# Transposing attention output and x1 by DMA instead of on TensorE, with the output projection moved ahead among the gates

## The reference, cut to what matters

```
h = x @ W_in + b_in                 # q | k | v | z | gate_attn | gate_gmlp
y_a = SWA_GQA(q, k, v, sinks) @ W_branch_attn
y_b = SGU(gelu(z)) @ W_branch_gmlp
mix = sigmoid(gate_attn) * y_a + sigmoid(gate_gmlp) * y_b
x1  = LayerNorm(alpha * x + mix @ W_out)
y   = LayerNorm(alpha * x1 + relu(x1 @ W_up)^2 @ W_down)
```

## Time and profile before

| | us |
|---|---|
| median of 3 runs | 1052.94 (1052.09 to 1054.36) |
| the profiled execution, slowest core's span | 1045.3 |
| the profiled execution, its own time | 1046.84 |
| spans of the 8 cores | 1043.9 to 1045.3 |
| mean granted TensorE clock of the cores | 0.994 to 0.996 |

### The profile page before, as it was taken

The page is one execution under the profiler, slowest core; times in us unless marked ns, Lnnn a source line. Parts: engine busy times, 40 slices in busy tenths (PEclk is TensorE's granted clock), DMA queues, the critical chain, the costliest instruction groups (busy, mean ns, idle before and its releaser), DMA issues.

```text
span 1045.3 us, 16998 instructions; the slowest of 8 cores (1043.9 to 1045.3 us)
## 1 busy us (share of the span) xinstructions
PE 1023.3 (98%) x6054; PEld 498.9 (48%) x6054; DVE 611.5 (59%) x1087; ACT 360.4 (34%) x484; POOL 89.1 (9%) x152
## 2 busy tenths in 40 slices
PE   8999999999999999999999999999999999999994
PEld 3446455554444444444444645555444444444442
DVE  2866477765876312336787827777486832133476
ACT  0454666651425200330024646666123430023100
POOL 4210000000111000000012000000010100010000
PEclk9999999999999999999999999999999999999998
DMA  9995234241797812953198222542156464086011
GB/s 160 188 174 95 41 53 98 54 102 33 150 162 150 142 20 35 166 82 82 61 185 149 50 41 44 91 102 51 61 124 138 75 129 80 1 134 108 21 61 80
DMA packets 20484, 98.65 MB, mean 94 GB/s; under 512 B 2353, under 2 KB 2993, under 8 KB 11954
## 3 DMA queue, kind: packets, MB, share of 16 engines
q0 software_dynamic: 13344, 73.41, 42.1%
q1 hardware_dynamic: 7058, 24.16, 6.8%
HBM read 162.57 MB, written 8.39 MB: 164 GB/s over the span
## 4 chain that ended last, share of the span: by engine, by line
PE 93%; DVE 3%; DMA 1%; issue 1%; ACT 1%; POOL 0%; DVEq 0%; POOLq 0%; ACTq 0%
PE ps L431 61%; PE ps L1147 20%; PE ps L924 3%; PE ps L674 2%; PE ps L942 2%; PE ps L889 2%; DMA ring<-wz 1%; PE ps L795 1%; DVE scr L392 1%; PE ps L972 1%; PE ps L1063 1%; PE ps L742 1%; DVE scr L897 0%; ACT scr L409 0%; DVE Cg L392 0%
## 5 line engine op out<-in xcount | busy, mean ns | idle before, releaser
L431 PE MATMUL ps<-reg,ring 128*128 128x512 bf16 x1536 | 344.7, 379 | 0.0
L431 PE MATMUL ps<-xT_s,ring 128*128 128x512 bf16 x1120 | 252.2, 375 | 0.2 <-DVE reg L392 0.2
L431 PEld LDWEIGHTS ps<-reg,ring 128*128 128x128 bf16 x1536 | 147.6, 98 | 172.7 <-issue 2.1
L1147 PE MATMUL ps<-ring,reg 128*128 128x512 bf16 x992 | 214.8, 379 | 0.0
L403 ACT ACTIVATE scr<-ps 128x512 f32<-128x512 f32 x128 | 76.4, 597 | 263.4 <-PE ps L431 260.0
L431 PEld LDWEIGHTS ps<-xT_s,ring 128*128 128x128 bf16 x1120 | 104.0, 98 | 115.0 <-issue 4.5
L392 DVE SCALAR_TENSOR_TENSOR reg<-ps,scr 128x512 bf16<-128x512 f32 x128 | 87.7, 690 | 113.8 <-ACT scr L403 113.7
L1147 PEld LDWEIGHTS ps<-ring,reg 128*128 128x128 bf16 x992 | 97.1, 98 | 117.0
L897 DVE CUSTOM_DVE_ANT_1 scr<-ps,masks 128x1024 f32<-128x1024 f32 x64 | 78.1, 1220 | 42.8 <-PE ps L889 34.9
L403 ACT ACTIVATE scr<-scr,amx 128x1024 bf16<-128x1024 f32 x64 | 73.2, 1144 | 15.9 <-DVE amx L392 11.8
L459 POOL DMA_DIRECT2D ring<-wst x62 | 34.6, 561 | 456.8 <-PE ps L431 165.2
(11 more groups left out here) (85 smaller groups left out, 722.7 us busy)
## 6 DMA issues: line engine op xcount, KB each, us to landing
ring<-wst POOLq DMA_DIRECT2D x62, 1024.0 KB, 10.7
regK<-x SPq DMA_DIRECT2D x16, 512.0 KB, 6.7
y<-scr SPq DMA_DIRECT2D x15, 512.0 KB, 2.6
lnbuf<-lnrep SPq DMA_DIRECT2D x4, 1024.0 KB
xT_s<-xt POOLq DMA_DIRECT2D x2, 1024.0 KB, 22.4
ring<-wz POOLq DMA_DIRECT2D x2, 1024.0 KB, 10.1
xT_s<-xt POOLq DMA_DIRECT2D x7, 256.0 KB, 19.3
ring<-wz POOLq DMA_DIRECT2D x7, 256.0 KB, 16.0
```

The source lines that it names most:

```text
L431: r = e.matmul(out, lhsT=a, rhs=b, start=(k == 0), stop=(k == 7))
L1147: r = e.matmul(ps[:, b2 + half, :], lhsT=hreg[fi // 8][:, th, fi % 8, bb * 128:(bb + 1) * 128], rhs=wd[quarter][:, fi % 4, half * 512:(hal ...
```

## The change: what it does

1. The 16 attention transposes and the 16 x1 transposes are taken off TensorE. Each is now one `dma_start_transpose` issued by SP, SBUF to SBUF, 256 KB (128 rows of 1024 bfloat16). The copies out of PSUM go too. Every such DMA waits for the one before it to complete (`turned[-1:]`), so that one at most is under way.
2. `ablk` and `x1T` are laid out so that a transfer has the form that the DMA wants; `up_unit` reads its moving operand as four pieces of 128 columns.
3. `o_A` of blocks 0 to 3 stands ahead of the gate of the same step, and `o_B`, `o_K`, `o_C` of the block before it directly behind that gate. The loop for blocks 4 to 7 is shorter and has 1 or 2 `up_unit`s in a step instead of 2, each behind `o_A` instead of ahead of it.
4. `load_x` of the next group stands behind all x1 transposes and waits for them.
5. The planner's landing time of every DMA that SP issues is bounded by its issue plus 2.0 plus three times its cost; before, all transfers were thought to share one line of traffic.

```diff
@@ schedule
                 wire = max(wire, at + 1.0) + o.cost
-                done[o] = max(wire, at + 2.2)
+                done[o] = max(wire if e == "pool" else min(wire, at + 2.0 + 3.0 * o.cost), at + 2.2)
...
+        def turn(dst, src, R, W, chan):
+
+            o = timed(P.op("sp", lambda e: e.dma_start_transpose(out=dst, in_=src), reads=R, writes=W, dma=True, chan=chan), 3.1)
+            o.deps.update(turned[-1:])
+            turned.append(o)
@@ att_A
-                timed(P.op("pe", f, reads=[B_ablk[bi], C["ident"]], writes=[B_ps[b]]), 0.45)
-                either(attnT[:, th, 2 * hk:2 * hk + 2, :], AT, [B_ps[b]], [B_at[th]])
+                turn(attnT[:, th, 2 * hk:2 * hk + 2, :].rearrange("p e (b q) -> p (e b) q", b=4),
+                     ablk[:, bi].rearrange("p e b c -> p (e b c)"), [B_ablk[bi]], [B_at[th][hk]], B_tp[bi])
@@ o_C
-                timed(P.op("pe", f, reads=bxb + [C["ident"]], writes=[B_ps[b]]), 0.45)
-                either(x1T[:, th, :, bb * 128:(bb + 1) * 128], XT, [B_ps[b]], [B_x1T[blk]])
+                turn(x1T[:, blk], xb, bxb, [B_x1T[blk]], B_tp[2 + blk % 3])
@@ the gates of half 1
             for e_ in range(8):
+                if e_ < 4:
+                    o_A(e_)
                 gate_unit("ga", e_, 1)
-                if 2 <= e_ < 6:
-                    o_K(e_ - 2)
+                if 1 <= e_ < 5:
+                    o_B(e_ - 1)
+                    o_K(e_ - 1)
+                    o_C(e_ - 1)
                 branch_unit("ga", e_, 1)
                 if e_ % 2 == 1:
                     release((g, "ga", e_ // 2))
-                if 0 <= e_ < 4:
-                    o_A(e_)
-                if 1 <= e_ < 5:
-                    o_B(e_ - 1)
-                if 3 <= e_ < 7:
-                    o_C(e_ - 3)
-            if g + 1 < NG:
-                load_x(g + 1, 0)
-                load_x(g + 1, 1)
-                load_x(g + 1, "h")
@@ blocks 4 to 7
-            for t in range(4, 12):
-                if t < 10:
-                    for _ in range(2):
-                        up_unit(0, *ups.pop(0))
+            for t in range(4, 9):
                 if t < NB:
                     o_A(t)
...
-                if 0 <= t - 5 < 4 and t >= 5:
+                for _ in range(1 + t % 2):
+                    up_unit(0, *ups.pop(0))
+                if t >= 5:
                     o_B(t - 1)
                     o_K(t - 1)
-                if t >= 10:
-                    for _ in range(2):
-                        up_unit(0, *ups.pop(0))
-                if 4 <= t - 3 < NB:
-                    o_C(t - 3)
+                    o_C(t - 1)
             if g + 1 < NG:
+                for part in (0, 1, "h"):
+                    load_x(g + 1, part, [b_.last_w for b_ in B_x1T])
```

More of the change, by code:

```diff
@@ L311, in build_program @@
         sgT = reg2
-        x1T = reg2
+        x1T = reg2[:].rearrange("p h e t -> p (h e t)").rearrange("p (b e t) -> p b e t", b=NB, e=8)
         attnT = reg3
@@ L330, in build_program @@
         B_ablk = [Buf("ablk%d" % i) for i in range(2)]
+        B_tp = [Buf("tp%d" % i) for i in range(5)]
         B_ln = Buf("ln")
@@ L482, in build_program, with load_x @@
         B_x = {"h": [Buf("xh")], 0: [Buf("x0_%d" % i) for i in range(4)], 1: [Buf("x1")]}
-        def load_x(g, part):
+        def load_x(g, part, after=()):
             dst = xp[part].rearrange("p k t -> p (k t)")
@@ L805, in group @@
             B_q = [[Buf("q") for _ in range(2)] for _ in range(8)]
-            B_at = [Buf("at0"), Buf("at1")]
+            B_at = [[Buf("at") for _ in range(4)] for _ in range(2)]
             if prev is None:
                 Prog.alias_after(B_ablk, [B_zero])
-                Prog.alias_after(B_at, [B_cst, B_tri, B_idf, C["ones"]])
+                Prog.alias_after(B_at[0] + B_at[1], [B_cst, B_tri, B_idf, C["ones"]])
             else:
                 for th in range(2):
-                    Prog.alias_after([B_at[th]], prev["h"][0][th])
+                    Prog.alias_after(B_at[th], prev["h"][0][th])
                     Prog.alias_after([b_[th] for b_ in B_q], prev["h"][1][th])
@@ L964, in att_A @@
                 bi = (t // 4) % 2
-                b = 2 + rot("ptb", 2)
-                AT = ps[:, b, :].bitcast(BF16).rearrange("p (e q) -> p e q", e=2)
-                def f(e):
-                    r = None
-                    for e2 in range(2):
-                        for b4 in range(4):
-                            r = e.transpose(out=AT[:, e2, b4 * 128:(b4 + 1) * 128], in_=ablk[:, bi, b4, e2 * 128:(e2 + 1) * 128], identity=identb[:])
-                    return r
-                timed(P.op("pe", f, reads=[B_ablk[bi], C["ident"]], writes=[B_ps[b]]), 0.45)
-                either(attnT[:, th, 2 * hk:2 * hk + 2, :], AT, [B_ps[b]], [B_at[th]])
+                turn(attnT[:, th, 2 * hk:2 * hk + 2, :].rearrange("p e (b q) -> p (e b) q", b=4),
+                     ablk[:, bi].rearrange("p e b c -> p (e b c)"), [B_ablk[bi]], [B_at[th][hk]], B_tp[bi])
             SK = 5
@@ L1056, in o_C @@
                 xb, bxb = oc[blk]
-                b = bank()
-                XT = ps[:, b, :].bitcast(BF16).rearrange("p (e t) -> p e t", e=8)
-                def f(e):
-                    r = None
-                    for e_ in range(8):
-                        r = e.transpose(out=XT[:, e_, :], in_=xb[:, e_ * 128:(e_ + 1) * 128], identity=identb[:])
-                    return r
-                timed(P.op("pe", f, reads=bxb + [C["ident"]], writes=[B_ps[b]]), 0.45)
-                either(x1T[:, th, :, bb * 128:(bb + 1) * 128], XT, [B_ps[b]], [B_x1T[blk]])
+                turn(x1T[:, blk], xb, bxb, [B_x1T[blk]], B_tp[2 + blk % 3])
             B_hT = [[[Buf("hT") for _ in range(2)] for _ in range(16)] for _ in range(2)]
```

21 lines of the change are left out of this document (12 added, 9 removed).

## The result

The changed kernel took 1082.26 us (median of 4 runs, 1071.05 to 1086.65) beside 1052.51 us (1051.53 to 1054.36) for the kernel before: ratio 1.027, 95% interval 1.0228 to 1.0311. The prediction said 1056.8 us, 1046 to 1072: slower is right, the size is not.

The account below looks back on a forecast made before the run. The prediction took TensorE's issue time plus its few waits as the bound: -14.1 + 2.6 + 3.6 + 10.8 + 1.0 = +3.9 us, added to the 1052.94 us median for 1056.8 us, range 1046 to 1072.

Parts of the forecast that it names:

- TensorE's time taken off: On TensorE, 32 transpose groups go at 0.44 us each, 14.1 us less in all.
- The start, +2.6: First projection starts 3.1 us late because `hgate` precedes the CASTs on VectorE; 0.5 us is given back later.
- the slow start: At the first matmuls, idle time might bring back a slow pace: up to 2.8 us on top, taken as 0.
- The wait for the last branch, 1.8 us twice: At block 4's output projection TensorE waits for VectorE's result of half 1's last branch, in both groups: +3.6 us.
- Attention, +1.0: In attention TensorE, with less to do, meets VectorE's results sooner: +1 us, bounds 0 and 3.
- The first up unit of half 1, +10.8: This unit waits for transposes of blocks 4 to 7: 7.3 us late in group 0, 3.5 in group 1.
- I take 5.0 us: Price of one 256 KB x1 transpose on SP, chosen from times of stores and loads; 2.5 us behind a load.
- The first half has room: Blocks 0 to 3: four transposes at 5 us end at 33 us, first up unit comes at 50, no wait.
- the sum: All terms from start to end of the kernel added together: +3.9 us.
- Rival 2: Each x1 transpose takes about 10.5 us, making half 1 late by 34 us over both groups: 1080 us, chance 0.13.
- rival 1: x1 transposes take 2 to 3 us, half 1 is late by 1 us or less: 1047.0 us, chance 0.27.
- Rivals 3 and 4: 3: VectorE paces attention, its 7 us return as waits, 1064 us, 0.05; 4: down weights late behind x, 1062 us, 0.09.

Follow-up runs that it names:

- e1: The kernel before, in its order, with only attention transposed by DMA and the bounded landing time for transposing transfers alone: 1042.1 us, ratio 0.9958.
- e3: The changed kernel with the planner's bounded landing time for transposing transfers alone, so the start has its old order: ratio 1.0361 to the kernel before.
- e8: The changed kernel's order, but x1 transposed on TensorE where its transfers stood; attention by DMA, bounded landing time for transposing transfers alone: ratio 0.9956.
- m3: No layer computed: 256 KB transposing transfers beside one, two or three steady ring loads, longest 8 to 11, 33 to 41, 46 to 54 us.
- e12: The changed kernel, but each ring load also waits for the one before it, so one at most is in flight: 1054.7 us, ratio 1.0074.
- m1: No layer computed: 256 KB transfers beside bunches of 0 to 3 ring loads; without a load 3.0 us transposing, 2.3 in rows, on core 4.
- m4: No layer computed: transposing transfers beside ring and residual loads, longest 37 to 45 us with TensorE and ScalarE idle, 24 to 54 with engines busy.
- e6: The changed kernel with x1's transfers made plain copies of the same bytes in 2 KB rows, not transposed: ratio 1.0053 to the kernel before.
- e7: The changed kernel with x1's transfers made plain copies of the same bytes in 256 B pieces, not transposed: ratio 1.0098 to the kernel before.

## Why the prediction was wrong, point by point

- **TensorE's time taken off: right.** 0.44 us per group; 7.1 us less busy for 16 groups in e1.
- **The start, +2.6: near.** The wait is 3.5 us on core 4 for 3.1 said, but TensorE began only 2.3 us late (12.47 for 10.19), and then the lower clock cost 1.5 us on the first 8 matmuls: the slow start for which the prediction gave a bound of 2.8 and took 0. At the DMA wait of 19.76 it is 3.1 us late (22.87). In e3 its removal gained nothing that the spread of x1's landings let be seen.
- **The wait for the last branch, 1.8 us twice: right**, 3.5 us in all. In e8 the planner fills it.
- **Attention, +1.0: near.** Waits for ScalarE and VectorE grew from 2.7 and 1.2 to 3.6 and 1.9 us on core 4, +1.6; with attention alone 2.6 of 7.0 us did not show in the time (e1).
- **The first up unit of half 1, +10.8: right in place, too dear.** On core 4 these waits are 2.9 and 1.6 us for 7.3 and 3.5 said, on core 7 3.7 and 2.1. Block 7's transfer took 3.1 to 3.4 us there, not 5.0.
- **"I take 5.0 us" and "The first half has room": the steps that failed.** The wait at the first up unit of the first half was put at nothing, from one price of 5.0 us for every transfer, taken from loads and stores. Measured in group 0 of the profiled execution it is 21.0, 20.4, 18.1, 13.6 and 6.9 us on cores 7, 5, 3, 1 and 2, and none on cores 0, 4 and 6. The room was as said: on core 7, 19 us from the issue of block 2's transfer (286.55) to the moment at which TensorE was ready (326.45 - 20.99), 17 in the prediction (33 to 50). The price was not: a transfer takes 3.0 us alone, 8 to 11 beside one load, and up to 33 to 54 beside steady streams of two or three (m3), and two or three ring loads are out with those of blocks 2 and 3 (at 283.8 and 290.7 us on core 3). The prediction's row for 14.3 us beside ring loads was kept as an upper bound, and it was the row nearest to this case. With the transfers of x1 at 3 to 11 us (e12) the wait in the first half is gone and the time is +0.74% for the sum's +0.37%. Why a landing crawls, and on which core, is open.
- **Rival 2 had the right time by luck, and half of the mechanism.** 1080 us for 1082.3, but by 10.5 us for every transfer and most of it in the second half. Of the 128 transfers of x1 on the eight cores 40 took up to 4 us, 79 took 4 to 13 and 9 took 16 to 37, and most of the waiting is in the first half. The Trainium skill's "VectorE: DVE Perf Modes", section "The three transpose paths", has 1309 ns for a 128x128 block; eight in one transfer take 3.0 us here, less than a third of the 10.5 worked out. The rule under rival 1, as fast as ordinary DMAs (the Trainium skill, "Advanced Engine Details and Errata", section "X-Bar Transpose (TRN2)"), nearly holds when alone (3.0 us for 2.3 in plain rows, m1) and fails beside three loads (46 to 54 us for 12 to 14 at most, m3).
- **Not thought of:** that cores would differ, and that a long wait is paid twice, as the matmuls behind it run at the lower clock: 5.6 us on core 7, of the 13.0 that a lower clock costs it.
- **Rivals 3 and 4:** 3 in part (above); no wait for down weights was seen in the changed kernel.

## What to carry to other kernels

Price a transfer in packets, not bytes alone: next to another queue's steady traffic it moved one packet for each of theirs, so 1056 packets of 256 B waited for some 1056 others. That is a price one can work out; the crawl isn't, and it cost more here. Both were small where one large load at most was in flight (8 to 11 us, m3; up to 10.8, e12), so there, and with slack over 11 us, is the place of a transposing DMA. Look at the span of every core first: when they fan out under one program in an undisturbed run, as here, a sum over one core's order won't give the time. Of a change with several parts, run each alone: here attention by DMA (0.9958), or with three of x1's blocks (0.9943, an interval that overlaps), beats both kernels.

## What the runs showed of the hardware that I had not expected

- A transposing transfer of 256 KB between SBUF tiles: 1056 packets, 1024 of them of 256 B, SP's issue 1.23 us (0.47 for a plain copy), up to 3.6 us in the kernel and 10.5 in m4 beside loads.
- The same transfer at the same instant took 5.1 us on one core and 31.0 on another, and held two ring loads at 28.6 and 30.5 us too.
- Beside a steady stream of three loads its packets and theirs went one for one (1041 to 1092 for 1056, m3), at 162 to 190 GB/s.
- At times all DMA traffic of a core crawls beside a transposing transfer, at 25 GB/s in the mean over 16 us on core 0 of m3, with nothing computed; the first transfer beside two steady loads went at 76 to 144 GB/s on every core there. From 280 to 306 us, where core 3 crawls, the cores of e6 and e7 moved 148 to 182 GB/s. Its cause is open.
- The granted clock of the changed kernel was below 1.00 in stretches in which TensorE was busy throughout (0.81 from 40 to 50 us on cores 4, 5 and 7, 0.86 and 0.85 from 570 to 590 us on core 7); what lowered it is open.
